# A hybrid decoder step on one core: the loop over eight turns reordered, and the past's suffix sums loaded as three bf16 parts and added by TensorE

## What is computed

```python
logf = log_sigmoid(f + f_bias)              # per token and head
F = cumsum(logf, axis=1)
s = einsum('nqhd,nkhd->nhqk', q, k) * HEAD_DIM ** -0.5
s = s + (Fq[:, :, :, None] - Fk[:, :, None, :])
p = softmax(where(kpos <= qpos, s, -inf))
o = einsum('nhqk,nkhd->nqhd', p, v)
x + (o * silu(z)) @ w_out
```

## Time and profile before

| | us |
|---|---|
| median of 3 runs | 928.37 (925.14 to 931.37) |
| the profiled execution | 924.18 |
| its span | 922.4 |
| TensorE busy in the span | 837.3 (91%) |
| VectorE busy | 545.6 (59%) |
| ScalarE busy | 342.4 (37%) |
| GpSimd busy | 217.3 (24%) |
| moved by DMA | 206.39 MB, mean 224 GB/s |

### The profile page before, as it was taken

How to read it: one execution, slowest core, us unless ns; L and a number is a source line. 1 busy time by engine, 2 the same in 40 slices (tenths; PEclk the granted TensorE clock), 3 DMA queues, 4 the chain that set the end, 5 groups by cost and what they waited for, 6 DMA issues and landing times.

```text
span 922.4 us, 22692 instructions
## 1 busy us (share of the span) xinstructions
PE 837.3 (91%) x8516; PEld 701.5 (76%) x8516; DVE 545.6 (59%) x1039; ACT 342.4 (37%) x728; POOL 217.3 (24%) x130
## 2 busy tenths in 40 slices
PE   3799999999998999698988988889888998897998
PEld 3799999999998899474765756567566675664998
DVE  4745565454436523747758578586695866946642
ACT  4333333332204444335345352452533525245210
POOL 2244333323211022213221321413223132130000
PEclk9999999999999999899999999999999999998999
DMA  7232323322554653298999999999999999994212
GB/s 212 69 88 72 91 70 89 91 68 91 140 137 122 238 178 120 71 365 267 315 370 299 376 349 318 395 317 379 366 329 397 292 381 391 312 402 140 92 46 104
DMA packets 148451, 206.39 MB, mean 224 GB/s; under 512 B 10527, under 2 KB 93136, under 8 KB 147266
## 3 DMA queue, kind: packets, MB, share of 16 engines
q1 hardware_dynamic: 138802, 199.40, 65.1%
q10 hardware_dynamic: 9088, 4.46, 1.6%
q0 software_dynamic: 528, 2.10, 0.8%
HBM read 195.29 MB, written 10.63 MB: 223 GB/s over the span
## 4 chain that ended last, share of the span: by engine, by line
PE 68%; DVE 14%; SPq 7%; issue 5%; DMA 4%; ACT 1%; DVEq 0%; POOL 0%; ACTq 0%; POOLq 0%
PE psum L1294 37%; PE psum L1320 10%; PE psum L1451 7%; DVE page_ring L1068 5%; SPq L387 4%; PE psum L1264 4%; PE psum L1558 3%; DMA page_ring<-in_cache_k 2%; PE psum L1491 1%; PE psum L1513 1%; DVE probs_odd L1138 1%; DMA w_raw<-in_a_w_in 1%; DMA w_raw<-in_a_w_out 1%; DVE tiny L1129 1%; DVE probs L1124 1%
## 5 line engine op out<-in xcount | busy, mean ns | idle before, releaser
L1294 PE MATMUL psum<-xn_high,w_high 128*128 128x256 f32 x992 | 226.8, 310 | 19.8 <-DVE page_ring L1068 16.9
L1294 PE MATMUL psum<-xn_low,w_high 128*128 128x256 f32 x992 | 213.6, 297 | 0.0
L1294 PE MATMUL psum<-xn_high,w_low 128*128 128x256 f32 x992 | 213.5, 297 | 0.0
L1294 PEld LDWEIGHTS psum<-xn_high,w_high 128*128 128x128 f32 x992 | 165.8, 191 | 52.8 <-issue 29.6
L1294 PEld LDWEIGHTS psum<-xn_high,w_low 128*128 128x128 f32 x992 | 168.2, 190 | 0.0
L1294 PEld LDWEIGHTS psum<-xn_low,w_high 128*128 128x128 f32 x992 | 168.1, 190 | 0.0
L1068 DVE STREAM_TRANSPOSE page_ring<-page_ring 128x1024 f32<-128x1024 f32 x128 | 149.5, 1215 | 6.2 <-DMA page_ring<-in_cache_k 5.6
L552 POOL TENSOR_TENSOR w_raw<-w_raw,gains 128x1024 f32<-128x1024 f32 x32 | 60.7, 1898 | 224.7 <-DMA w_raw<-in_b_w_in 213.4
L914 DVE TENSOR_TENSOR w_low<-w_raw,w_high 128x1024 fp32r<-128x1024 f32 x32 | 50.4, 1576 | 77.4 <-ACT w_high L630 77.4
L561 POOL TENSOR_TENSOR w_low<-w_raw,w_high 128x1024 fp32r<-128x1024 f32 x22 | 52.4, 2380 | 131.4 <-ACT w_high L681 131.4
L529 POOL TENSOR_TENSOR w_raw<-w_raw,gains 128x1024 f32<-128x1024 f32 x30 | 61.9, 2063 | 86.9 <-DMA w_raw<-in_a_w_in 86.9
(11 more groups left out here) (243 smaller groups left out, 1431.8 us busy)
## 6 DMA issues: line engine op xcount, KB each, us to landing
page_ring<-in_cache_k SPq DMA_DIRECT2D x256, 256.0 KB, 6.2
page_ring<-in_cache_v SPq DMA_DIRECT2D x128, 512.0 KB, 9.6
w_raw<-in_a_w_in SPq DMA_DIRECT2D x32, 512.0 KB, 4.0
sample_scores<-suffix_scratch SPq DMA_DIRECT2D x8, 1024.0 KB, 12.4
w_raw<-in_b_w_in SPq DMA_DIRECT2D x16, 512.0 KB, 6.0
w_raw<-in_kv_w SPq DMA_DIRECT2D x16, 512.0 KB, 8.9
w_raw<-in_a_w_out SPq DMA_DIRECT2D x4, 1024.0 KB, 4.8
f_broad<-f_scratch SPq DMA_DIRECT2D x8, 512.0 KB, 7.6
```

The costliest lines, as they stand in the source:

```text
L1294: mm = pe.matmul(PS[:, bank + h, 0:c.stop - c.start], w[:, k, :], x[:, k, c], start=(k == 0 and n == 0), stop=(k == KT - 1 and n == 2))
```

## The change

It has three parts.

1. *Suffix sums.* After L1001 they are split in three bf16 parts (ScalarE rounds, VectorE subtracts the rounded part, twice) and stored as `[8, 3, 16, 2048]` in bf16 by 24 transfers. Turn i loads one `[48, 2048]` bf16 tile `SUF`. `EACH` is a 48 x 128 matrix of zeros and ones that gives head h's three parts to the eight rows of head h. Sixteen matmuls per turn write the sums into the four score banks ahead of `past_scores(0)`, which adds to them. VectorE takes one maximum over 2048 elements of PSUM, and ScalarE's exponentials read PSUM and write `SS`.
2. *Work moves between engines.* The three low parts of a turn go from GpSimd to VectorE. The three stores of new keys and values go from ScalarE's queue to SyncE's, behind value page 15; that page now waits until the rows of keys and values are copied.
3. *Orders.* TensorE turns the key rows before the last piece of project(1), into OP and OS instead of T0 and T1, and the value rows after the first two pieces of project(2). `block_scores(0)` waits for all four exponentials. Pieces 5, 6, 7 of project(2) stand one place earlier. VectorE divides block 0 before the maximum of block 1, and block 3 before it turns a key page of the next turn.

The diff, its core:

```diff
-    suffix_dram = nc.dram_tensor("suffix_scratch", [NB, H, PAST], F32, kind="Internal").ap()
+    suffix_dram = nc.dram_tensor("suffix_scratch", [NB, 3, H, PAST], BF16, kind="Internal").ap()
...
         def load_suffix(b):
-            src = suffix_dram[bass.ds(b, 1), :, :].rearrange("a h n -> (a h) n")
-            sp.dma_start(SS[:, :], src.unsqueeze(1).to_broadcast([H, NQ, PAST])).then_inc(b_sfx, 16)
+            sp.dma_start(SUF[:, :], suffix_dram[bass.ds(b, 1), :, :, :].rearrange("a t h n -> (a t h) n")).then_inc(b_sfx, 16)
...
                 if n % 8 == 0:
                     sp.wait_ge(b_scored, 2 * i + n // 8 + 1)
+                if n == NPG - 1:
+
+                    sp.wait_ge(b_t0f, 8 * i + 2)
+                    sp.wait_ge(b_t1f, 8 * i + 2)
                 load_values(pages, n)
...
+            cols = bass.ds(i * P, P)
+            sp.dma_start(k_prompt[0].rearrange("(t p) h d -> p t (h d)", p=P)[:, :, cols], KN[:, 0:QB, :]).then_inc(b_kpo, 16)
+            sp.dma_start(v_prompt[0].rearrange("(t p) h d -> p t (h d)", p=P)[:, :, cols], VN[:, :, :]).then_inc(b_vpo, 16)
+            sp.dma_start(k_sample.rearrange("b q h d -> (b q) (h d)")[:, cols], KN[0:NS, QB, :]).then_inc(b_kso, 16)
...
-        pool.wait_ge(s_sfx, 1)
-        for b in range(NB):
-            pool.dma_start(suffix_dram[b].rearrange("h (g n) -> g h n", g=NPG),
-                           CS[b * NPG:(b + 1) * NPG, :, :]).then_inc(s_sfx_st, 16)
+        for t in range(3):
+            pool.wait_ge(s_sfp, t + 1)
+            for b in range(NB):
+                pool.dma_start(suffix_dram[b, t].rearrange("h (g n) -> g h n", g=NPG),
+                               CSB[t][b * NPG:(b + 1) * NPG, :, :]).then_inc(s_sfx_st, 16)
...
         def heads(i, last):
             scale_b(1, 6 + 2 * i, G_B)
-            low_b(KT + 3 * i + 2, 1)
             pool.wait_ge(b_rr, i + 1)
             pool.tensor_tensor(KN_T[:, :], KN_T[:, :], RR[:, :], ALU.mult).then_inc(b_normed, 1)
             if not last:
                 scale_b(0, 6 + i, G_KV)
-                low_b(KT + 3 * i + 3, 0)
...
-                low_b(KT + 3 * i + 4, 1)
...
+            if n == 1:
+                act.wait_ge(s_sfx, 1)
+
+                for t in range(3):
+                    if t:
+                        act.wait_ge(s_sfr, t)
+                    act.activation(CSB[t][:, :, :], CS[:, :, :], ACT.Copy).then_inc(s_sfp, 1)
...
-            for c in range(4):
-                if c == 2:
-                    turned0(VN[:, :, :], PS[:, T0, :].rearrange("p (k n) -> p k n", k=4)).then_inc(b_t0f, 1)
-                ins = act.activation(SS[:, c * 512:(c + 1) * 512], SS[:, c * 512:(c + 1) * 512], ACT.Exp,
-                                     bias=TINY[:, 13:14], accum_out=TINY[:, 16 + c:17 + c])
-                ins.then_inc(b_es, 1)
+            for g in range(4):
+                ss = SS[:, :].rearrange("p (n g k) -> p n g k", g=4, k=32)[:, :, g, :]
+                act.activation(ss, PS[:, T0 + g, :].rearrange("p (n k) -> p n k", k=32), ACT.Exp,
+                               bias=TINY[:, 13:14], accum_out=TINY[:, 16 + g:17 + g]).then_inc(b_es, 1)
...
+        for t in range(2):
+            dve.wait_ge(s_sfp, t + 1)
+            dve.tensor_tensor(CS[:, :, :], CS[:, :, :], CSB[t][:, :, :], ALU.subtract).then_inc(s_sfr, 1)
...
-            for g in range(4):
-                ss = SS[:, :].rearrange("p (n g k) -> p n g k", g=4, k=32)[:, :, g, :]
-                dve.tensor_tensor_reduce(ss, PS[:, T0 + g, :].rearrange("p (n k) -> p n k", k=32), ss,
-                                         1.0, NEG, ALU.add, ALU.max, TINY[:, 4 + g:5 + g]).then_inc(b_taken, 1)
-            dve.wait_ge(b_taken, 4 * i + 4)
...
-            ch.link(dve.tensor_reduce(TINY[:, 14:15], TINY[:, 4:8], AX, ALU.max))
+            ch.link(dve.tensor_reduce(TINY[:, 14:15], PS[:, T0:T0 + 4, :].rearrange("p a n -> p (a n)"), AX, ALU.max))
...
+            block_divide(0)
             block_max(1)
-            block_divide(0)
             block_turned(0)
             block_max(2)
             block_divide(1)
+            if not last:
+                low_b(KT + 3 * i + 4, 1)
...
+            block_divide(3)
             if not last:
                 turn_keys(i + 1, 0)
-            block_divide(3)
...
-            project(0, range(KT - 1))
+            project(0, range(KT - 2))
...
+            pe.wait_ge(b_sfx, 16 * (i + 1))
+            project(0, [KT - 2])
+            for g in range(4):
+                for j in range(4):
+                    pe.matmul(PS[32 * j:32 * j + 32, T0 + g, :].rearrange("p (n k) -> p n k", k=32),
+                              EACH[:, 32 * j:32 * j + 32],
+                              SUF[:, :].rearrange("p (n g k) -> p n g k", g=4, k=32)[:, :, g, :],
+                              start=True, stop=False, tile_position=(0, 32 * j))
...
+            pe.wait_ge(b_ln, i + 1)
+            pe.wait_ge(b_normed, i + 1)
+            rows_turned(KN_T)
             pe.wait_ge(b_turned, NPG * i + NPG)
             project(1, [KT - 1])
             past_scores(1)
...
-            pe.wait_ge(b_taken, 4 * i + 4)
+            project(2, [2, 3, 4])
+            pe.wait_ge(b_es, 4 * i + 4)
             pe.wait_ge(b_qt, i + 1)
             block_scores(0)
```

More of the change, by code:

```diff
@@ L198, in build @@
     CS = place("logf_sums", [P, H, PAGE], over=at["sample_scores"])
+    CSB = [place(f"suffix_part{t}", [P, H, PAGE], BF16, over=o) for t, o in enumerate(
+        (at["o_past"], at["o_past"] + 2 * H * PAGE, at["new_keys"]))]
+    SUF = place("suffix", [3 * H, PAST], BF16, over=at["sample_scores"])
     STN = place("state_rows", [2 * NB, D], over=at["new_keys"])
@@ L817, in heads @@
             block_turned(0)
+            if not last:
+                act.wait_ge(b_proj, KT + 3 * i + 3)
+                high_b(KT + 3 * i + 4, 1)
             block_exp(2)
@@ L822, in heads @@
             block_turned(2)
-            if not last:
-                high_b(KT + 3 * i + 4, 1)
             act.wait_ge(b_zm, i + 1)
@@ L1173, in heads @@
             if not last:
-                turn_keys(i + 1, 2)
-                turn_keys(i + 1, 3)
+                for n in range(1, 4):
+                    turn_keys(i + 1, n)
             assert t1[0] == 8
```

81 lines of the change are left out of this document (40 added, 41 removed).

## The result

The changed kernel takes 972.77 us (median of 4 runs, 968.26 to 973.75), the kernel before 928.41 beside it; the ratio is 1.0469, interval 1.042 to 1.0518. The forecast was 947 with a range to 965: the direction is right, the size is not, and the time lies outside the range.

What follows compares the result with a forecast made beforehand. Before the change TensorE bounds the turn, VectorE just behind; after it Z's circle does. First interval 63.1 plus six of 60.4 is +15.7, ends +4.3: 928.4 + 20 = 948, rounded down to 947; range 927 to 965.

Steps and rivals of the forecast that it cites:

- Z's circle: Per turn, S (end of past scores' second half) to S through gate weights Z's issue, landing and use: 60.4 us.
- Z's issue moves from S + 35.0 to S + 36.5: On SyncE, the three stores moved there delay the issue of the gate's weights Z from S + 35.0 to S + 36.5.
- I take 7.2: In the transfer queue, Z lands 7.2 us after its issue (6.9 to 8.3), against 13.1 before.
- 16.7 from landing to the scores: From Z's landing: scaling, rounding, subtraction and transposes 6.84, project(1)'s last piece 1.1, scores 4.4; given as 16.7 us together.
- Rival 1: TensorE's clock falls in front of the scores: +2.0 a turn, 62.4 us a turn, 961 in all; chance 0.15.
- The suffix load: In the transfer queue, the load shrinks from 1,049 to 197 KB and costs 0.5 us of it.
- Rival 3: The suffix load gets no cheaper, Z lands after 13.1: a circle of 66.3, 988 in all; chance 0.03.
- Rival 4: TensorE's sixteen suffix matmuls run singly, 3.8 instead of 1.0 us: path 60.5, 948 in all; no chance given.
- The wait for the exponentials: TensorE waits 2.5 us before block_scores(0) and should lose full clock: half speed for some 3.3 us costs 1.6.
- TensorE's own path, 57.7: TensorE's turn with costs added and saved waits removed: 57.7 us, or 59.3 with the clock's loss, under 60.4.
- Rival 2: Z lands within 4.4 us of issue, VectorE never stands, TensorE sets the turn: 926, or 938 with clock loss; chance 0.22.
- Ends: Outside the seven intervals: output projection +1.2, key rows before the first S +0.6, last turn +2.5; +4.3 in all.

Runs made afterwards that it cites:

- e1: The changed kernel with VectorE's low part of the gate's weights Z moved from between key pages 9 and 10 to behind page 15: 960.02 us, ratio 1.0398.
- e7: The kernel before, with only the low part of the gate's weights Z moved to VectorE, between key pages 9 and 10: 980.09 us, ratio 1.0616.
- e5: The changed kernel with the three stores back on ScalarE's queue, behind its last copy of turned probabilities: 934.5 us, ratio 1.0106.
- e9: The changed kernel with only the third store (the sample's keys, 64 rows of 512 bytes) back on ScalarE's queue: ratio 1.0305.
- e3: The changed kernel with the load of the gate's weights Z issued behind the keys of slot 4: 973.91 us, ratio 1.0547.
- e6: The changed kernel with the stores back on ScalarE's queue, the suffix load behind slot 0 and Z's load behind slot 4: 916.28 us, ratio 0.9882.
- e11: The changed kernel with the stores back on ScalarE's queue and Z's load behind slot 4: 914.88 us, ratio 0.9842.
- e8: The kernel before, with only the three stores moved to SyncE behind value page 15, which waits for the copies: 980.64 us, ratio 1.0601.
- e12: e6 with two more pieces of project(2), 5 and 6, ahead of TensorE's wait for the exponentials: 896.94 us, ratio 0.9673.

## Why the prediction was right and wrong, step by step

- **What bounds it.** Right. S to S is set by Z's circle: SyncE, landing, GpSimd, ScalarE, VectorE, TensorE. In all seven turns the chain runs through GpSimd's work on Z, the rounding, the transposes and the scores, in the last of them through Z's transfer too. e1 broke the circle, and e7 made it in the kernel before. Two more circles of nearly the same length stood beside it.
- **"Z's issue moves from S + 35.0 to S + 36.5".** This step failed. The forecast for the seven intervals was 425.5 us, 60.8 each; they took 458.0, 65.4 each, in pieces 37.9 + 10.4 + 17.2 where a settled turn was reckoned as 36.5 + 7.2 + 16.7. Without the 1.5 us for the stores the forecast would have been 59.3 each, and e5 measured 59.7. So the stores cost 5.8 us a turn (65.4 - 59.65), and of the 4.6 us by which the circle was short 4.3 are theirs. The price was read from ScalarE's queue, where they stand alone. On SyncE's, behind 4 MB of value pages, they hold it for 6.2 by e5, 3.9 of it in the third by e9. Rows 4 had the warning: an issue stuck for 6.35 us, because the queue was full, was in the prediction's first part and not in this term. In the turn shown Z's issue stands at S + 38.2, not at 35.0 + 6.2 = 41.2, since the value pages and the keys behind the small suffix load are now issued faster (18 halves, the suffix and 10 more took 16.6 us up to Z instead of 18.3; value pages 8 to 15 took 3.92 instead of 5.23).
- **"I take 7.2" for Z's landing.** It took 10.6 from issue to GpSimd's start, 10.4 in the mean. The queue was not slower than reckoned: from the landing of the first group's last half, at 632.70 + 8.1 = 640.8, 0.2 + 10 x 0.262 + 0.524 = 3.34 MB took 9.3 us, 360 GB/s, inside the 340 to 402 and near the 8.7 us that it used. What was wrong is the start and the end of that stretch. The prediction gave this last half the median landing of three, 6.7; the last of them alone took 8.1, and it did so before the change too. And SyncE issues ten halves in 5.26 us now, not 6.52, so Z is issued sooner behind the same bytes; time won at the issue comes back in the landing. Issue and landing together were priced at 43.7 and took 48.8: 3.1 because the last half is issued later (S + 31.4, not 28.3), 1.4 for its landing, 0.6 for the stretch behind it. The sign "no stuck issue of 6 us" held only in part: the four key halves behind Z take 6.17 us to issue.
- **16.7 from landing to the scores.** 18.1 in this turn, 17.2 in the mean: 16.5 or 16.6 in four turns of seven, 17.9 or 18.0 in three. The steps to the last transpose were right (11.1, as reckoned); the rest, partly at half speed, took 1.45 and 5.53 instead of 1.1 and 4.4. Rival 1, a clock that falls in front of the scores, had this mechanism and gave it 2.0 a turn; measured is 1.4 here and 0.5 in the mean, and it came on top of the late Z, not instead. e5 has the same 17.2, so it is no part of what the stores cost.
- Sum of the turn shown: 38.2 + 10.6 + 18.1 = 66.9 against 60.4; it took 66.83. The first turn took 66.6 against 63.1.
- **The suffix load.** The prediction priced its bytes in the queue and never TensorE's wait for it. Issued at S + 32, landed 8.2 later, it stopped TensorE 5.33 us before the sixteen products, at half clock after that. It did not set this turn (VectorE was free at 650.26 and Z's rounding came at 653.1), but 2.85 us of slack is all that was left, and e1 and e3 ran into it. The stores stand in this circle too. Rival 3, a suffix load that gets no cheaper in the queue, is refuted: the suffix load itself lands after 8.2 us, the half ahead of it after 8.1, Z after 10.5 and not 13.1.
- **The sixteen products.** "4 x 0.24 = 1.0" was right at full clock: all sixteen take 1.04 us in e5. At half clock they take 1.89, as in the turn shown. Rival 4, one by one for 3.8, is refuted:

```profile
643.37 1.89 PE L1485 MATMUL psum<-suffix,each_head 48*32 48x512 bf16 x16
...
625.38 1.04 PE L1483 MATMUL psum<-suffix,each_head 48*32 48x512 bf16 x16
```

- **The wait for the exponentials.** 2.5 predicted, 15.2 over seven turns or 2.2 each measured. "A wait of 2.5 should lose" the clock did not hold in the turn shown: after 1.81 us it stayed at 1.00.
- **TensorE's own path, 57.7.** Near: with Z and the stores out of the way e6 and e11 run at 57.2 and 57.1. Behind its slow first turn of 61.9, e11's turns take 55.8 to 56.8. Rival 2, Z in time and not slower than before, needed a landing within 4.4 us. e11 met its condition by issuing Z eleven microseconds sooner, and the time came out at 0.984.
- **Ends.** +1.8 at the head was +0.6; +2.5 in the last turn was -1.1. In the output projection VectorE did come 1.5 us later to its first norm (287.12 instead of 285.65 in the chains), the rest was caught up by the first S. Small beside the 48 us.

Open is why e8's turn, 66.8 us, lies above the 61 to 63 that was expected: 2.6 of it is the later start of the keys (S + 24.1 instead of 21.5), and for the rest half clock behind the waits is in the trace, but no run separates it. Open is also how full a queue must be before a store sticks.

## What to carry to other kernels

- Price a step on the queue that it is moved to, not on the one that it comes from: put its issues behind what stands there, count an issue behind megabytes as one that can stick, and move the start of everything after it. Three stores of 1.5 us held SyncE for 6.2 and cost 5.8 us a turn.
- An operation that waits for a late load should not stand in the middle of an engine's order. If it must, pull its load ahead of the bulk; moving one load helps only when the other circles through the same queue have slack too.
- Read the landing of the transfer that the sum starts from, not the median of its neighbours, and take the mean of the turns beside the one turn that is shown.
- When a wait is removed and nothing is won, read which wait is next and test the moves together.

## What the runs showed of the hardware that was not expected

- A store of 64 rows of 512 bytes kept SyncE 4.29 us, the same store 0.50 on ScalarE's queue; the stores ahead of it, eight times its size each, 0.81 and 0.55.
- The 192 KB suffix load lands 4.3 us after its issue (median) with two key halves ahead of it (e12), 8.2 behind the keys; 512 KB on a nearly empty queue took 4.0. The Trainium skill (SBUF — State Buffer, Door 1) would have a load into 48 partitions run at half the rate. The row does not speak against that, but no run loads the same bytes into 128 partitions, so it stays open.
- What the stores cost came by way of the queue that issues them. The Trainium skill (DMA: Bandwidth & Descriptors, Issuing engines are not separate DMA queues) calls the time that a second issuing engine saves "usually small relative to the DMA itself". Here it was not small: the bytes are the same in e5 and in the changed kernel, the issuing engine and with it the moment of issue differ, and that is 6.2 us of SyncE and 5.5 us of the mean turn.
- TensorE's granted clock did not follow the length of the last wait alone. It stayed at 1.00 behind 1.81 us; in e5 it read 0.66 and 0.50 behind 2.27, and after a 1.85 us wait in the changed kernel 0.65 and 0.50:

```profile
607.00:609.00 2.00, 1.15 (x10) 0.77 (x11) 0.00 (x0) 0.80 (x4) 0.00 (x0) 1.00 1.01 395
...
595.00:597.00 2.00, 1.65 (x8) 0.99 (x8) 0.00 (x0) 0.30 (x2) 0.00 (x0) 0.66 1.00 385
```

The first row is the changed kernel's, the second e5's; 0.66 is the mean of a stretch that is partly at full speed (1.00, 2.4 GHz) and partly at half (0.50, 1.2 GHz). Half clock is worth a term of its own: TensorE's mean clock is 0.989 before, 0.950 in the changed kernel and 0.992 in e12, whose turns have no wait over 1.3 us.
